# Two of nine token tiles take all experts as dense products instead of gathered rows

## The reference, cut to what matters

```python
# 1024 prompt tokens + 64 sample tokens, D_MODEL 1024; before this: norm, projection, GLA, window attention, merge
def peer_ffn(xn, w_q, keys1, keys2, u, v):            # u, v: (16384, 1024) f32
    q = (xt @ w_q).reshape(n, 8, 2, 128)
    s1 = einsum('nhd,hkd->nhk', q[:, :, 0], keys1); s2 = einsum('nhd,hkd->nhk', q[:, :, 1], keys2)
    v1, i1 = top_k(s1, 16); v2, i2 = top_k(s2, 16)
    cand = v1[..., :, None] + v2[..., None, :]        # 256 pairs per head
    top_s, sel = top_k(cand, 16)
    idx = take(i1 * 128 + i2, sel)                    # 8 heads x 16 = 128 experts per token
    g = softmax(top_s)
    act = gelu(einsum('pd,ped->pe', xb, u[idx]))
    return einsum('pe,ped->pd', g * act, v[idx])
h = h + peer_ffn(rmsnorm(h)); y = rmsnorm(h)
```

## Time and profile before

| | us |
|---|---|
| median of 3 runs (4152.72 to 4165.62) | 4153.2 |
| the profiled execution | 4136.31 |
| its span | 4134.5 |
| PE busy in the span (74%) | 3062.2 |
| DVE busy (59%) | 2434.9 |
| POOL busy (57%) | 2361.4 |
| ACT busy (17%) | 717.4 |
| DMA: 1463.50 MB, mean | 354 GB/s |

### The profile page before, as it was taken

One profiled execution on the slowest core, in us unless ns is written; L12 is line 12 of the kernel. 1 busy time (PEld: TensorE's weight loads), 2 busy tenths in 40 slices (PEclk: granted clock), 3 DMA queues, 4 the chain that ended last, 5 costly groups with the idle time before them and its releaser, 6 DMA issues.

```text
span 4134.5 us, 40085 instructions
## 1 busy us (share of the span) xinstructions
PE 3062.2 (74%) x14004; PEld 1685.2 (41%) x14004; DVE 2434.9 (59%) x6237; ACT 717.4 (17%) x1573; POOL 2361.4 (57%) x2188
## 2 busy tenths in 40 slices
PE   8988448789967669878985767698965666656667
PEld 7877337677723236546762312244510000000111
DVE  3332893376778836357667856465566666665540
ACT  5451220243323200124221210000100000000000
POOL 0000341255667846456666766666677777777775
PEclk9999569899978789989996777698987777777999
DMA  4537878789999999899999999999999999999999
GB/s 151 170 127 275 259 236 304 250 326 414 414 344 378 352 374 410 327 348 397 413 412 349 369 354 401 386 408 412 412 397 409 409 409 406 409 407 373 409 409 351
DMA packets 458657, 1463.50 MB, mean 354 GB/s; under 512 B 52568, under 2 KB 139672, under 8 KB 438088
## 3 DMA queue, kind: packets, MB, share of 16 engines
q0 software_dynamic: 313344, 1140.99, 71.1%
q1 hardware_dynamic: 145112, 319.95, 21.3%
HBM read 1390.83 MB, written 71.11 MB: 354 GB/s over the span
## 4 chain that ended last, share of the span: by engine, by line
PE 33%; DMA 27%; POOL 21%; issue 8%; DVE 7%; ACT 2%; SPq 2%; POOLq 0%; DVEq 0%; ACTq 0%
DMA e_v_rows<-in_v,e_expT 18%; POOL e_v_rows L1849 11%; POOL e_u_rows L1839 10%; PE e_o_ps L2137 7%; PE O L1746 6%; PE X L1711 5%; DVE e_u_rows L2053 3%; PE X L1728 1%; PE X L848 1%; DMA jb_w<-in_w_big 1%; PE X L850 1%; PE X L849 1%; PE e_o_ps L848 1%; DMA n_st<-in_state 1%; PE e_o_ps L850 1%
## 5 line engine op out<-in xcount | busy, mean ns | idle before, releaser
L1839 POOL DMA_INDIRECT e_u_rows<-in_u,e_expert x1024 | 1122.1, 1096 | 1139.1 <-DVE e_dots L2053 477.0
L2137 PE MATMUL e_o_ps<-e_v_rows,e_zw 128*32 128x512 f32 x4352 | 1241.5, 766 | 580.3 <-DMA e_v_rows<-in_v,e_expT 567.0
L2053 DVE CUSTOM_DVE_ANT_0 e_u_rows<-e_u_rows,e_xn 128x1024 f32<-128x1024 f32 x1088 | 1325.8, 1219 | 548.9 <-DMA e_u_rows<-in_u,e_expert 427.7
L1849 POOL DMA_INDIRECT e_v_rows<-in_v,e_expT x1088 | 1174.2, 1079 | 597.2 <-PE e_o_ps L2137 317.1
L2137 PEld LDWEIGHTS e_o_ps<-e_v_rows,e_zw 128*32 128x32 f32 x4352 | 210.1, 124 | 1484.0 <-DMA e_v_rows<-in_v,e_expT 1142.4
L1746 PE MATMUL O<-f_oaT,f_ring 128*128 128x384 f32 (+2 forms) x1024 | 265.4, 414 | 2.4 <-issue 1.5
L802 DVE TENSOR_TENSOR jb_wl<-jb_w,jb_wh 128x512 fp32r<-128x512 f32 (+1 forms) x200 | 131.8, 687 | 183.7 <-ACT jb_wh L725 183.5
L1746 PEld LDWEIGHTS O<-f_oaT,f_ring 128*128 128x128 f32 x1024 | 176.6, 196 | 78.6 <-issue 12.2
L1711 PE MATMUL X<-f_oaT,f_ring 128*128 128x384 f32 (+2 forms) x512 | 135.9, 420 | 26.8 <-DMA f_ring<-in_w_feed 19.9
L725 ACT ACTIVATE jb_wh<-jb_w 128x512 fp32r<-128x512 f32 (+1 forms) x200 | 120.6, 628 | 160.6 <-PE X L850 66.4
L1711 PE MATMUL X<-f_obT,f_ring 128*128 128x384 f32 (+2 forms) x512 | 133.0, 414 | 17.9 <-DMA f_obT<-ob_cols 17.9
(11 more groups left out here) (312 smaller groups left out, 4539.9 us busy)
## 6 DMA issues: line engine op xcount, KB each, us to landing
f_ring<-in_w_feed SPq DMA_DIRECT2D x80, 1024.0 KB
jb_w<-in_w_big SPq DMA_DIRECT2D x48, 1024.0 KB, 8.7
ja_w<-in_w_big SPq DMA_DIRECT2D x24, 1024.0 KB, 5.1
e_v_rows<-in_v,e_expT POOLq DMA_INDIRECT x1088, 9.5
e_u_rows<-in_u,e_expert POOLq DMA_INDIRECT x1024, 9.6
z_feat<-jb_stage SPq DMA_DIRECT2D x64, 192.0 KB
e_sc<-scores SPq DMA_DIRECT2D x36, 256.0 KB, 6.5
z_feat<-ja_stage SPq DMA_DIRECT2D x32, 192.0 KB
```

Source lines behind the costliest of these rows:

```text
L1839: pool.indirect_dma_start(u_ring[:, count % U_RING, :], None, u_dram, bass.IndirectOffsetOnAxis(ap=index, axis=0)).then_inc(u_got[count % ...
L1849: pool.indirect_dma_start(v_ring[:, count % V_RING, :], None, v_dram, bass.IndirectOffsetOnAxis(ap=expT[:, t % 2, n:n + 1], axis=0)).then_ ...
L2053: dve.tensor_tensor_reduce(u_ring[:, count % U_RING, :], u_ring[:, count % U_RING, :], xn[:, t % 2, :], 1.0, 0.0, ALU.mult, ALU.add, dots[ ...
L2137: last = pe.matmul(o_ps[32 * j:32 * (j + 1), cols], zw[:, part % 2, j, hot_col:hot_col + 32], v_ring[:, (first + j) % V_RING, cols], start ...
```

## The change

Tiles 4 and 5 leave the gathered order; the gathered positions are now tiles 0, 1, 2, 3, 6, 7, 8. Their experts are still selected on DVE, two heads in some slots. After feed 3 a dense part works on their 256 tokens at once, in two halves of 64 key columns:

- Build: for each token ACT makes a one-hot of 64 first keys (Abs, then Relu of 1 - |difference|) and DVE one of 128 second keys times the gate weight; two products on PE give the token's 64 x 128 gate weights, eight tokens to a PSUM bank, which ACT copies into `W.A`.
- 64 steps: SP loads 128 rows of u (transposed on the host) and of v, 512 KB each; PE takes eight products with 256 tokens, ACT gelu, DVE scales with `W.A`, and PE adds four products with v into X and O, where they stay for all 128 steps.
- Finish: residual, norm and store of both tiles.

The rings fall from eight buffers to seven, the pitch of the slots becomes 2.9, 3.9 from slot 128 and 3.5 from 512, two stretches change, `iota` grows to 128 columns. u and v also lie in HBM a second time in the dense order.

```diff
-SLOT_US = 2.90
+PITCH = ((0, 2.9), (128, 3.9), (512, 3.5))
+DENSE = (4, 5)
+GATHERED = [t for t in range(TILES) if t not in DENSE]
+END = len(GATHERED)
+DN = P * len(DENSE)
+WIN = 64
+D_RING = 3
+STEP_US, BUILD_US = 7.6, 0.55
+TURN, BATCH = 4, 8
...
-    U_RING, V_RING = 8, 8
+    U_RING, V_RING = 7, 7
...
+        def dense_fill(r, sb):
+            r.A = sb("d_A", [P, WIN, DN])
+            r.xT = sb("d_xT_sb", [P, KT, DN])
+            r.u = sb("d_u", [P, D_RING, D])
+            r.v = sb("d_v", [P, D_RING, D])
...
+        d_ps = U[:, 0:DN]
+        d_built_ps = U[:, :].rearrange("p (t j) -> p t j", t=BATCH)
+        d_acc = [X, O]
...
-        stretches = (1.3, 1.05, 1.05, 1.25)
+        stretches = (1.3, 1.05, 1.1, 1.15)
...
+        DENSE_FROM, DENSE_UNTIL = 20, 30
+        for p in range(1, END + 1):
+            g = feed_of(tile_of(p))
+            if g != feed_of(tile_of(p - 1)):
+                late = p * HEADS == DENSE_UNTIL + 2
+                first = (p * HEADS - (0 if late else 2)) * TOPK
+                need = scored(g, 1) + (26.0 if late else 8.0) - at_slot(first)
+                if need > 0:
+                    gaps.append((first, need))
...
+        dense_at = scored(FEEDS - 1, HEADS - 1) + 16.0
+        def build_at(w, n):
+            return dense_at + (WIN * STEP_US + 8.0) * w + BUILD_US * DN * w + BUILD_US * n
+        def step_at(s):
+            return build_at(s // WIN, DN) + 4.0 + STEP_US * (s % WIN)
...
+        def dense_rows(sp):
+            yield dense_at - 2.0
+            after_feed(sp, FEEDS - 1)
+            sp.wait_ge(out_copied, 16 * 7)
+            sp.dma_start(W.xT[:, :, :], d_xT).then_inc(d_x_in, 16)
...
+        def dense_weights(sp):
+            for s in range(2 * WIN):
+                yield dense_at + 1.0 + s if s < D_RING else step_at(s - D_RING) + STEP_US - 2.0
+                if s == 0:
+                    sp.wait_ge(d_x_in, x_in_0 + 16)
+                wait(sp, d_g_done, g_done_0 + s - D_RING + 1)
+                sp.dma_start(W.u[:, s % D_RING, :], i_("u_dense")[s]).then_inc(d_u_in[s % D_RING], 16)
+                yield dense_at + 1.5 + s if s < D_RING else step_at(s - D_RING) + 2 * STEP_US
+                wait(sp, d_o_done, o_done_0 + s - D_RING + 1)
+                sp.dma_start(W.v[:, s % D_RING, :], i_("v_dense")[s]).then_inc(d_v_in[s % D_RING], 16)
...
+        def dense_rows_dve(dve):
...
+                    wait(dve, d_built, built_0 + DN * w + n - TURN + 1)
+                    dve.tensor_scalar(d_wj[:, n % TURN, :], iota[:, :], d_slot[:, 1, n:n + 1], d_slot[:, 2, n:n + 1],
+                                      ALU.is_equal, ALU.mult).then_inc(d_wj_ready, 1)
+        def dense_cols_act(act):
...
+                    act.activation(d_oi[:, n % TURN, :], window_cols(w), ACT.Abs, bias=d_slot[:, 0, n:n + 1]).then_inc(d_abs, 1)
+                    act.wait_ge(d_abs, abs_0 + count + 1)
+                    act.activation(d_oi[:, n % TURN, :], d_oi[:, n % TURN, :], ACT.Relu, bias=keep[:, 0, 1:2], scale=-1.0
+                                   ).then_inc(d_oi_ready, 1)
+                    if n % BATCH == BATCH - 1:
+                        yield build_at(w, n) + 2.2
+                        act.wait_ge(d_built, built_0 + count + 1)
+                        wait(act, d_h_ready, h_ready_0 + WIN * w)
+                        act.activation(W.A[:, :, n - BATCH + 1:n + 1].rearrange("p j t -> p t j"),
+                                       d_built_ps[:, :, :], ACT.Copy).then_inc(d_a_taken, 1)
+        def dense_build(pe):
...
+                    if n % BATCH == 0:
+                        wait(pe, d_a_taken, a_taken_0 + count // BATCH)
+                        wait(pe, d_act_ready, act_ready_0 + WIN * w)
+                    pe.wait_ge(d_wj_ready, wj_ready_0 + count + 1)
+                    pe.wait_ge(d_oi_ready, count + 1)
+                    for part in range(2):
+                        last = pe.matmul(d_built_ps[part * WIN:(part + 1) * WIN, n % BATCH, :],
+                                         d_oi[:, n % TURN, :], d_wj[:, n % TURN, part * WIN:(part + 1) * WIN],
+                                         start=True, stop=True)
+        def dense_products(pe):
+            for s in range(2 * WIN):
+                yield step_at(s)
...
+                pe.wait_ge(d_u_in[s % D_RING], 16 * (s // D_RING + 1))
+                wait(pe, d_act_ready, act_ready_0 + s)
+                for k in range(KT):
+                    last = pe.matmul(d_ps, W.u[:, s % D_RING, k * P:(k + 1) * P], W.xT[:, k, :],
+                                     start=(k == 0), stop=(k == KT - 1))
+                last.then_inc(d_g_done, 1)
+        def dense_gelu(act):
...
+                wait(act, d_h_ready, h_ready_0 + s - 1)
+                act.activation(d_act[:, s % 2, :], d_ps, ACT.Gelu).then_inc(d_act_ready, 1)
+        def dense_scale(dve):
...
+                dve.tensor_tensor(d_H[:, s % 2, :], d_act[:, s % 2, :], W.A[:, s % WIN, :], ALU.mult).then_inc(d_h_ready, 1)
+        def dense_sums(pe):
+            for s in range(2 * WIN):
+                yield step_at(s) + STEP_US + 0.1
+                pe.wait_ge(d_h_ready, h_ready_0 + s + 1)
+                pe.wait_ge(d_v_in[s % D_RING], 16 * (s // D_RING + 1))
+                for i in range(len(DENSE)):
+                    for half in range(2):
+                        cols = slice(half * BANK, (half + 1) * BANK)
+                        last = pe.matmul(d_acc[i][:, cols], d_H[:, s % 2, i * P:(i + 1) * P], W.v[:, s % D_RING, cols],
+                                         start=(s == 0), stop=(s == 2 * WIN - 1))
+                last.then_inc(d_o_done, 1)
...
```

More of the change, by code:

```diff
@@ L535, in layer_stage, with pitch @@
         gaps = []
+        def pitch(p):
+            return [us for first, us in PITCH if p >= first][-1]
         def at_slot(p):
[L538 to L551 removed]
@@ L573, in feed_of, with tile_of @@
+            return start + us + sum(extra for first, extra in gaps if p >= first)
+        def tile_of(p):
+            return GATHERED[p] if p < END else LAST
         def feed_of(t):
             return [g for g in range(FEEDS) if t in FEED_TILES[g]][0]
+        DENSE_FROM, DENSE_UNTIL = 20, 30
[7 more added lines that the diff above has]
+                    gaps.append((first, need))
@@ new lines, in dense_turn @@
+        def dense_turn(pe):
+            for i in range(len(DENSE)):
+                for what in range(3):
+                    yield dense_turn_at(i) + 0.5 + 1.5 * what + (2.0 if what == 2 else 0.0)
+                    if what == 2:
+                        pe.wait_ge(d_w_ready, i + 1)
+                        src = d_gate[:, :, :]
+                    else:
+                        pe.wait_ge(d_picked, HEADS * (i + 1))
+                        src = d_keys[:, what, :, :]
+                    wait(pe, d_turn_taken, 3 * i + what)
+                    pe.transpose(d_tr[:, :], src.rearrange("p h k -> p (h k)"), ident[:, :]).then_inc(d_turned, 1)
@@ new lines, in dense_turn_act @@
+        def dense_turn_act(act):
+            for i in range(len(DENSE)):
+                for what in range(3):
+                    if what == 2:
+                        yield dense_turn_at(i) + 1.0
+                        act.wait_ge(d_gate_in, i + 1)
+                        act.activation(d_gate[:, :, :], d_gate[:, :, :], ACT.Exp).then_inc(d_gate_exp, 1)
+                    yield dense_turn_at(i) + 0.8 + 1.5 * what + (2.5 if what == 2 else 0.0)
+                    act.wait_ge(d_turned, 3 * i + what + 1)
+                    act.activation(d_slot[:, what, i * P:(i + 1) * P], d_tr[:, :], ACT.Copy,
+                                   scale=-1.0 if what == 0 else 1.0).then_inc(d_turn_taken, 1)
@@ L1897, in finish_act @@
         def finish_act(act):
-            for t in range(LAST + 1):
+            for t in range(END + 1):
                 n = tokens(t)
@@ L1978, in select @@
             chain.settle()
+            if dense:
+                dve.tensor_reduce(d_keys[:, :, h, :], hot[:, :, :, :], AX_X, ALU.add).then_inc(d_picked, 1)
+                dve.wait_ge(d_picked, HEADS * DENSE.index(tile) + h + 1)
+                return
             chain.step(dve.tensor_reduce(picked[:, :, :], hot[:, :, :, :], AX_X, ALU.add))
@@ L2032, in expert_dve, with chained @@
         def expert_dve(dve, chain):
+            def chained(units):
+                for unit in units:
+                    yield from unit
             def finished(steps):
@@ L2063, in expert_dve @@
                     finished(gating)
-            yield at(LAST + 1, 0, 1)
-            weights(dve, chain, LAST)
+            yield at(END + 1, 0, 1)
+            weights(dve, chain, END)
         def finish_dve(dve, chain):
-            for t in range(LAST + 1):
+            for t in range(END + 1):
                 n = tokens(t)
@@ L2110, in expert_turns @@
         def expert_turns(pe):
-            for t in range(LAST + 1):
-                yield at(t, 6, 8 if t < LAST else 5)
```

(2 more changed lines are left out.)

358 lines of the change are left out of this document (278 added, 80 removed).

## The result

The changed kernel takes 4357.3 us (median of 4 runs, 4354.8 to 4360.7) where the kernel before takes 4154.0 beside it: ratio 1.048, 95% interval 1.046 to 1.050. It is 4.8% slower; the forecast was 0.8% faster (4122 us), and the time lies above the range of 3960 to 4280.

What follows compares the result with a forecast made beforehand. Transfers, near 410 GB/s, were taken as the bound. Front 2631 + dense input 10 + builds 330 + steps 1094 + half ends 14 + finish 25 = 4104 us span, scaled to 4122; range 3960 to 4280, own band 4040 to 4166.

Steps and rivals of the forecast that it cites:

- The queues interleave 2.9/3.9 as many gathers with the same front work: Front after 805 us: 25.6% fewer gathers beside unchanged work, so feed 3 ends at 2631 us instead of 3022.
- the floors: Front stages after 805 us: remaining bytes at each stage's own rate, 1637 us in all; 2217 if nothing gained.
- The builds, 165 us each: Dense part after feed 3: two builds of 256 tokens at 165 us each, ends 145 and 215.
- nearest to ACT's row: Builds: 165 us chosen close to ACT's 161 us, from 0.63 us per token, with DVE's 141 us under it.
- The steps, 1094 us: Dense part's 128 steps: 8.5 us each at 389 GB/s, 1094 us, ends 1047 and 1183.
- fall together: Dense steps: PE's limit of 1047 us and the transfers' 1039 us coincide, so neither is reached.
- Ring of seven: Rival for the dense steps: seven buffers delay v rows, 1225 us instead of 1094, total 4253 us; chance 0.23.
- The front keeps its length: Rival up to feed 3: stages did not wait for removed gathers, feed 3 ends at 2745, total 4236 us; chance 0.10.
- The faster rival: Front falls to 2530, builds to ACT's 0.6, steps to PE's 1047: 3947 us; chance 0.20 for below 4040.
- some 200 us: Gathers' rest in feed 3, until tile 6 is scored: bandwidth goes unused, the price of this order.
- The signs of being wrong: Forecast counts as wrong if feed 3 ends later than 2750 us or a dense step takes over 9.5 us.

Runs made afterwards that it cites:

- e16: Changed kernel with each gather behind the first seven of a ring bringing an eighth of its bytes, every instruction and wait kept; 4154 us.
- e1: Kernel before the change with both rings used modulo seven instead of eight buffers, nothing else; 4201.8 us, ratio 1.013.
- e6: e5 with ACT besides doing two Abs and then two Relu, two tokens at a time; 4304.6 us, ratio 1.039.
- e5: Changed kernel with ACT's gate copy behind the next three tokens' one-hots and gates laid out token by token, so the copy writes in a row; 4300.0 us.
- e2: Changed kernel with half of the first four f32 products' work per dense step left out, transfers and waits kept; 4309.6 us.
- e3: Changed kernel loading only the first three blocks of u and v and computing all dense steps from them; 4331.9 us.
- e12: e5 with 0.9 us planned per build token, dense operands rounded to one-pass f32, and rings of two blocks; 4240.1 us, ratio 1.022.

## Why the prediction was wrong, point by point

**"The queues interleave 2.9/3.9 as many gathers with the same front work", and the floors.** This step failed, by 98 us. I took each stage's bytes at its own rate as its length where the DMA line was full, "the projections are the fullest, so their floors hold nearly: 270 and 306". They took 317 and 329; feed 2 322 for 295, feed 3 309 for 275. The mixing stages and the sample, which I had judged by their chains, came out as forecast or shorter (259 for 280, 198 and 189 for 200 each). A full DMA line says that transfers are busy, not that the stage waits for them. A view that the prediction doesn't use says so: how long PE waited for v rows in the kernel before (total us, times, longest), in the two projections, feed 2 and feed 3.

```profile
PE e_o_ps L2137 <- DMA e_v_rows<-in_v,e_expT: 9.3, 4, 4.0
PE e_o_ps L2137 <- DMA e_v_rows<-in_v,e_expT: 37.7, 17, 5.1
PE e_o_ps L2137 <- DMA e_v_rows<-in_v,e_expT: 2.8, 3, 1.9
PE e_o_ps L2137 <- DMA e_v_rows<-in_v,e_expT: 27.8, 17, 4.0
```

PE's sums fell by 7.6, 43.1, 4.8 and 66.8 us in the four (39.9 to 32.3, 84.6 to 41.5, 46.9 to 42.1, 85.6 to 18.8), and the stages shrank by 9, 46, 9 and 73: hardly more than the work that left PE. e16 shows what bytes could have given. Measured from feed 2 to its last product, the second projection took 370 us before, 320 after, and 298 with seven eighths of the row bytes gone; the forecast had taken 69 us off for a quarter of the gathers. Up to 38 us of the 98 may be the ring's, since seven buffers cost the kernel before as much up to feed 3 (e1); no run has the changed kernel with eight. Feed 3 shows another miss: I gave it PE's 268 us and 7 more. PE was busy 257 us there but idle 52, as it waits some 30 us for its first rows, before and after alike (f_xn from oa_rows, 23.7 and 25.1 us, and what follows it).

**The builds, 165 us each.** They failed by 132 us, and with them the choice of "nearest to ACT's row": both stayed above even the upper end of 215 us. ACT's 128x64 took 0.33 and 0.35 us, not 0.239. The Trainium skill, "ScalarE: Activation LUTs", section "What ACT_TABLE_LOAD costs", gives 186 ns + 0.833 ns a column with immediate scale and bias and about 93 ns more for each [128,1] pointer operand, 239 and 333 ns for 64 columns. The trace agrees within 5%: 239, 330 and 348 here. But the build did not pay for these durations as such: in e6 the same operations last 0.33 us and yet start 0.24 apart, the forecast's own price, since neighbours overlap. In the changed kernel each Relu waits for its Abs, and a token's pair takes 0.62 us from start to start: +36 us a build. The copy took 1.04 us, not 0.595: +14. And it stands ahead of the next token's operations, so that ACT waits 39 us for PE where I had put 19. The dependent pair and the strided write stand on no row I had read; e6 and e5 show them.

**The steps, 1094 us.** Right to 2% with their ends, and in part by luck: the 1094 came from a transfer rate of 389 GB/s, and the second half ran at 353 with PE as its limit. The two limits did "fall together" in the first half (e2 and e3), at 8.35 us a step; but both were reached there, and in the second, at 9.25, PE alone was. PE was busy 1106 us, not 1047: the v rows 211 where I had 278 x 0.48 = 133, and what is left, 895, the dense products (914 forecast). There were 337 v rows, as v runs a tile behind u, and the last tile's rows fill only two column strips: 16 instructions took 3.63 us there in place of 1.92.

**Ring of seven.** Real, at 53 us in the kernel before, but not where the rival had put it: in the steps PE waited 10.1 and 10.8 us in all for v rows.

**The front keeps its length.** This rival, to which I gave 0.10, had feed 3 at 2745 and was nearly right. Its reason, that the removed gathers were not what the stages waited for, holds for their bytes; their sums on PE did count, 260 of the 293 us gained. Its 4236 lacked little but the builds' 132.

**The faster rival** fell with all its parts, floors, builds and steps. **The "some 200 us" of unused bandwidth** were seen: feed 3 ran at 215 GB/s and the builds at 213 and 202. What they cost is another matter, for e16 shows that the builds hardly wait for bytes (224 and 227 us there).

**The signs of being wrong.** Neither came, with feed 3 at 2729 (2750 was the bound) and a step at 9.25 us (9.5), though the span was 252 us off: there was no such bound on a build, the largest miss.

The error under all of these is one: I saw that the kernel was full of transfers, and counted what the change takes from them, while PE, busy 78% of the front, had little room. The dense part brings PE 895 us of products and the builds' besides; what left PE up to feed 3 are 260 us of sums. Nor does 0.48 us hold for a v row in general: it is that of four taken at once, and in the front before 606 rows took 534 us (2426 instructions, four a row), 0.88 each.

## What to carry to other kernels

A nearly full DMA line is not a bound: before a stage is shortened by its bytes, read what its busiest compute engine waits for, and count on little more than those waits and the removed work; here no more came. A change that trades bytes for dense f32 products needs the price of both on the engine that gets them; taking the bytes away on the chip (an eighth of each row) answers in one run whether there was anything to gain. Price a new short operation from start to start, and from a row with the same surroundings (strided output, a semaphore from the operation just ahead), for a loop of 512 of them multiplies what the row leaves out.

## What the runs showed of the hardware

- ACT writing 128x512 from PSUM with a stride of 1 KB between elements took 1.04 us, in a row 0.58. DVE reading 128x256 with a stride of 256 bytes took 0.60 us in place of 0.43 (e5).
- In the builds the granted clock fell to 0.57 to 0.58 (0.99 in the steps around them), mostly the 1.2 GHz level, with PE busy 144 of 227 us in short products and idle up to 1.7 us at every eighth token. The same 16 instructions on four v rows took 3.64 us there and 1.92 in the steps.
- An f32 product took 3.3 times as long as one of operands rounded to the one-pass form (3.45 and 1.05 us for eight of 256 columns). The Trainium skill, "FP8 and Floating Point Precision", section "TensorE Precision Notes", speaks of four passes for f32; the trace shows a little less, which no run here divides further.
- Two dependent ACTIVATEs of 64 columns, Abs and then Relu of the same token, took 0.62 us from start to start, and 0.48 where two tokens were interleaved (e6).
- Gathers and block loads together moved 400 to 406 GB/s over more than 500 us (first steps of the kernel after, e2 and e12), as gathers alone do.
